# Two transformer blocks on one core: turning order at two norms, turning of memory tokens, pairs in the spatial mixing, and the queue of the modulation loads

## The reference

```python
for layer in range(2):
    mod = silu(c) @ ada_w[layer] + ada_b[layer]           # six rows of 1024
    sh1, sc1, g1, sh2, sc2, g2 = split(mod, 6)
    h = modulate(rmsnorm(x, norm_mix[layer]), sh1, sc1)
    y = retention_mixer(h, ...) if layer == 0 else sgu_mixer(h, ...)
    x = x + g1 * y
    h = modulate(rmsnorm(x, norm_ffn[layer]), sh2, sc2)
    x = x + g2 * peer_ffn(h, ...)
```

## Time and profile before

| | us |
|---|---|
| median of 3 runs | 2386.43 |
| lowest and highest | 2381.01, 2391.15 |
| the profiled execution | 2387.99 |
| its span in the profile | 2386.2 |
| PE busy | 2008.0 (84%) |
| DVE busy | 1578.9 (66%) |
| ACT busy | 1012.5 (42%) |
| POOL busy | 652.3 (27%) |

### The profile page before, as it was taken

How to read it: one execution, slowest core, us unless ns; L and a number is a source line. 1 busy time by engine, 2 the same in 40 slices (tenths; PEclk the granted TensorE clock), 3 DMA queues, 4 the chain that set the end, 5 groups by cost and what they waited for, 6 DMA issues and landing times. The chain is left out here.

```text
span 2386.2 us, 23881 instructions
## 1 busy us (share of the span) xinstructions
PE 2008.0 (84%) x8016; PEld 1248.9 (52%) x8016; DVE 1578.9 (66%) x2973; ACT 1012.5 (42%) x2119; POOL 652.3 (27%) x642
## 2 busy tenths in 40 slices
PE   3998879877877788899877988888878888989998
PEld 2976665322222233379655544434333336868997
DVE  6875766766667676578665766676677655555654
ACT  2342344444444444345333443544454444344543
POOL 0011023443434434110002434443444440400000
PEclk9999999999999999999998999999999999889999
DMA  6785669999999999787455989999999995323553
GB/s 277 285 302 195 218 264 421 421 421 422 421 421 420 422 421 418 295 304 266 148 201 195 421 369 422 411 421 417 421 418 417 421 421 196 124 99 122 184 187 141
DMA packets 112633, 761.92 MB, mean 319 GB/s; under 512 B 12880, under 2 KB 13664, under 8 KB 26368
## 3 DMA queue, kind: packets, MB, share of 16 engines
q0 software_dynamic: 88240, 591.62, 60.8%
q1 hardware_dynamic: 23312, 165.78, 18.8%
q10 hardware_dynamic: 960, 3.01, 0.4%
HBM read 759.32 MB, written 1.05 MB: 319 GB/s over the span
## 5 line engine op out<-in xcount | busy, mean ns | idle before, releaser
L837 PE MATMUL pair<-uv,p_diag 128*128 128x512 f32 x1536 | 755.0, 627 | 188.3 <-ACT p_diag L2005 187.8
L1416 DVE CUSTOM_DVE_ANT_0 uv<-uv,p_h 128x1024 f32<-128x1024 f32 x384 | 470.3, 1225 | 351.2 <-DMA uv<-in_peer_uv,p_idx 350.9
L494 POOL DMA_INDIRECT uv<-in_peer_uv,p_idx x384 | 430.5, 1121 | 721.1 <-PE pair L837 592.2
L837 PEld LDWEIGHTS pair<-uv,p_diag 128*128 128x128 f32 x1536 | 278.1, 195 | 640.1 <-ACT p_diag L2005 377.7
L1084 DVE TENSOR_TENSOR ring_low<-ring,ring_high 128x2048 fp32r<-128x2048 f32 x148 | 336.5, 2288 | 146.5 <-ACT ring_high L1820 144.0
L1820 ACT ACTIVATE ring_high<-ring 128x2048 fp32r<-128x2048 f32 x148 | 278.8, 1908 | 217.0 <-DMA ring<-in_ret_w_in 52.6
L1999 ACT ACTIVATE p_act<-p_dot 128x1 f32<-128x1 f32 x512 | 103.1, 201 | 612.3 <-DVE p_dot L1416 611.0
L642 PE MATMUL pair<-hT_high,ring_high 128*128 128x256 f32 x1056 | 303.9, 288 | 4.7 <-DVE hT_low L1094 3.4
L642 PE MATMUL pair<-hT_low,ring_high 128*128 128x256 f32 x1056 | 298.7, 283 | 0.0
L642 PE MATMUL pair<-hT_high,ring_low 128*128 128x256 f32 x1056 | 298.7, 283 | 0.0
L837 PE MATMUL pair<-uv_high,p_diag 128*128 128x512 f32 x512 | 250.3, 620 | 48.8 <-ACT p_diag L2005 45.0
(11 more groups left out here) (345 smaller groups left out, 2393.1 us busy)
## 6 DMA issues: line engine op xcount, KB each, us to landing
ada<-in_ada_w POOLq DMA_DIRECT2D x50, 512.0 KB, 5.3
ring<-in_ret_w_in SPq DMA_DIRECT2D x24, 1024.0 KB, 6.7
ring<-in_sgu_w_in SPq DMA_DIRECT2D x24, 1024.0 KB, 6.2
ring<-in_peer_w_query SPq DMA_DIRECT2D x16, 1024.0 KB, 4.8
ring<-in_w_up SPq DMA_DIRECT2D x16, 1024.0 KB, 4.9
ring<-in_w_down SPq DMA_DIRECT2D x16, 1024.0 KB, 4.8
mod<-in_ada_w POOLq DMA_DIRECT2D x30, 512.0 KB, 6.4
ring<-in_sgu_w_out SPq DMA_DIRECT2D x12, 1024.0 KB, 4.8
```

What stands on the lines that cost most here:

```text
L494: nc.gpsimd.indirect_dma_start(uv_rows[SLOT[l][s]].rearrange("p a d -> p (a d)"), None, experts, bass.IndirectOffsetOnAxis(ap=p_idx[:, k:k ...
L837: mm = nc.tensor.matmul(acc[:, half, :], p_diag[:, n % DIAGS, :], v[:, half * 512:(half + 1) * 512], start=(k == 0), stop=(k == PICKS - 1))
L1416: V.tensor_tensor_reduce(out=u, in0=u, in1=p_h[:, s // PICKS, :], scale=1.0, scalar=0.0, op0=ALU.mult, op1=ALU.add, accum_out=p_dot[:, n % ...
```

## The change

- In norms 1 and 3 DVE makes the low parts of tile 0 ahead of its wait for tile 1's root (`finish_tile`), and ACT takes tile 0's groups between the roots of tile 0 and tile 1. `FILL` loses its entries for norms 1 and 3. `keep_running` now comes before the first tile of a `turn_rows` call that holds tile 1; this moves the fillers of norm 0 ahead of tile 0.
- The memory tokens are turned at s = 41 (tile 0) and s = 47 (tile 1); ACT takes them at s = 43 and 49, DVE lowers them at s = 44 and 50.
- PE makes a memory block at the ninth step of its unit instead of the first. ACT's high of the later block moves from the start of the unit to k = 10, DVE's low from k = 9 to k = 13.
- In the mixing DVE does the sum and product of b and b + 1, then both low parts, then one ring low. The ring block named at odd b is (b + 1) // 2, at even b it was b // 2 + 1.
- The 80 modulation loads are issued by SP after ring loads that `loaded_after` names: piece j after the ring block two behind the one that goes before the sum of piece j - 3 (j - 2 from piece 48 on). The waits of `load_ada` itself stay.

```diff
+MEM_AT = (41, 47)
-FILL = {0: 3, 1: 3, 2: 4, 3: 3, 5: 6}
+FILL = {0: 3, 2: 4, 5: 6}
...
+        taken_after = []
+        for c in range(12):
+            for n, count in enumerate((0, 0) if c == 0 else (1, 1) if c < 4 else (1, 2) if c < 10 else (2, 2)):
+                taken_after += count * [2 * c + 2 + n]
+        taken_after += 8 * [25] + [26 + n // 2 for n in range(8)]
+        for c in range(12):
+            taken_after += [first_block_of[("sgu_v", 6)] + 2 + 2 * c + n for n in range(2)]
+        taken_after += [first_block_of[("sgu_out", 1)] + 2 + n // 2 for n in range(8)]
+        loaded_after = collections.defaultdict(list)
+        for j in range(len(ADA_AT)):
+            ahead = 3 if j < 6 * KD else 2
+            start = R - 1 if j < 6 * KD else first_block_of[("sgu_v", 6)] + 3
+            loaded_after[max(start, taken_after[j - ahead] + 2 if j >= ahead else 0)].append(j)
...
                 sp.dma_start(ring[:, i % R], blocks[i]).then_inc(w_in[i % R], 16)
+                for j in loaded_after[i]:
+                    if j == 6 * KD:
+                        sp.wait_ge(x_ready, norm_count(2, 1))
+                    load_ada(sp, j)
...
                     load_gain_and_bias(v)
-                    for j in range((v - 2) * KD, (v - 1) * KD):
-                        load_ada(pool, j)
...
+                if TT - 1 in tiles:
+                    keep_running(("hT", n, tiles[0], 0), FILL.get(n, 0))
                 for t in tiles:
-                    if t == TT - 1:
-                        keep_running(("hT", n, t, 0), FILL.get(n, 0))
...
-                        turn_rows(6, m_h)
+                    if l == 1 and s in MEM_AT:
+                        turn_rows(6, m_h, (MEM_AT.index(s),))
...
-                    if l == 1 and s % TOPK == 0 and 0 <= j < 8:
+                    if l == 1 and s % TOPK == TOPK // 2 and 0 <= j < 8:
                         memory_block(j // 2, j % 2)
...
             def finish_tile(n, t, h, shift):
+                if n in (1, 3) and t == 1:
+                    lows_hT(n, ((0, 0), (0, 1)))
...
-                    if b:
-                        us_low(b - 1)
                     dve.wait_ge(small_ready, SMALL[name] + 1)
...
-                    if b >= 2 and b % 2 == 0:
-                        lows(first_block_of[("sgu_out", 0)] + b // 2 + 1)
-                us_low(CU // 2 - 1)
+                    if b % 2:
+                        us_low(b - 1)
+                        us_low(b)
+                        lows(first_block_of[("sgu_out", 0)] + (b + 1) // 2)
...
-                for t in range(TT):
-                    last_half_root(1, t)
+                last_half_root(1, 0)
+                take_hT(1, ((0, 0), (0, 1)))
+                last_half_root(1, 1)
```

More of the change, by code:

```diff
@@ L1420, in peer @@
                 n = 1 + 2 * l
-                lows_hT(n)
+                lows_hT(n, ((1, 0), (1, 1)))
                 first = query_first[l]
@@ L1448, in peer @@
                         if s == 40:
-                            if l == 1:
-                                lows_hT(6)
                             lows(first + 9)
-                        if k == late and l == 1 and KV_UNIT <= i < KV_UNIT + 8:
+                        if l == 1 and s - 3 in MEM_AT:
+                            t = MEM_AT.index(s - 3)
+                            lows_hT(6, ((t, 0), (t, 1)))
+                        if k == 13 and l == 1 and KV_UNIT <= i < KV_UNIT + 8:
                             lows(kv_first + i - KV_UNIT + 2)
@@ L1959, in peer @@
                 n = 1 + 2 * l
-                take_hT(n)
+                take_hT(n, ((1, 0), (1, 1)))
                 def exponentials(i):
@@ L1991, in peer @@
                         did(A.activation(dst, pair[kv_pair][:, :, :], ACT.Copy), kv_taken, c + 1)
-                    if l == 1 and KV_UNIT <= i < KV_UNIT + 8:
-                        highs(kv_first + i - KV_UNIT + 2)
                     for k in range(TOPK):
@@ L2016, in peer @@
                                 take_mod(11)
-                                take_hT(6)
                             highs(first + 9)
+                        if l == 1 and k == 10 and KV_UNIT <= i < KV_UNIT + 8:
+                            highs(kv_first + i - KV_UNIT + 2)
+                        if l == 1 and s - 2 in MEM_AT:
+                            t = MEM_AT.index(s - 2)
+                            take_hT(6, ((t, 0), (t, 1)))
                         if s == EXIT_AT:
@@ L2059, in sgu @@
                     high_of(s_us[0][:, 2 * b:2 * b + 2, :], s_t[:, 4 + 2 * (b % 2):6 + 2 * (b % 2), :])
-                    if b >= 2 and b % 2 == 0:
-                        highs(first_block_of[("sgu_out", 0)] + b // 2 + 1)
+                    if b % 2:
+                        highs(first_block_of[("sgu_out", 0)] + (b + 1) // 2)
                 highs(block_after(("sgu_out",), 0))
@@ L2066, in sgu @@
                 load_keys(1)
-                for t in range(TT):
-                    last_half_root(3, t)
+                last_half_root(3, 0)
+                take_hT(3, ((0, 0), (0, 1)))
+                last_half_root(3, 1)
             def hybrid():
```

## The result

The changed kernel ran at 2359.54 us (median of four, 2355.3 to 2366.3) beside 2385.59 us for the kernel before: ratio 0.9892, 95% interval 0.9860 to 0.9925, so 26 us less. Timed again with the experiments it had 2357.55 us (2355.3 to 2360.6) beside 2387.76, ratio 0.9868 [0.9850, 0.9887], 30 us less. The forecast was 2354.5, in the range 2340 to 2373. The profiled execution took 2357.6 us (span 2355.7).

The account below looks back on a forecast made before the run. Two DMA-bound expert phases with dense stages around them, where PE multiplies or waits for DVE's low parts. 9.9 + 12 + 6 + 1 + 3 = 32 off the profiled 2388, less 1.6 to the median: 2354.5 us, range 2340 to 2373.

Parts of the forecast that it names:

- Part 1: Norms 0, 1 and 3: tile 0's low parts made early, fillers gone; 4.5 plus 2.7 twice, 9.9 us gained.
- PE starts near 47.7 and warm: Norm 0: PE's first product starts near 47.7 instead of 52.67, at full clock; 4.5 us of 5.0 taken.
- Part 2: Mixing in pairs: 8.15 us a pair on DVE instead of 9.87, 7.8 on PE; 12 us gained.
- Part 3: Second expert phase, step 36: memory tokens turned tile by tile remove the 213 GB/s hole; 6 us gained.
- Part 4: Memory blocks at mid-unit: ACT waited 30.4 us for PE's block, DMA lost little; 1 us gained.
- Part 5: 80 modulation loads moved from POOL's to SP's queue: 3 us gained, ends -10 and 6.
- Start of sgu ... Net gain 2: Gating unit's start: the two first modulation rows load with the norm, crowding the bias loads; net 2 us gained.
- step for the last sgu_u chunks: Last sgu_u chunks: ring loads wait 2.3 us later behind rows, absorbed by the ring's lead; 0, ends -1 and 8.
- gain of 2 in sgu_out: Second half of sgu_out: row 76 follows one ring block and lands 2 us earlier, shortening DVE's and PE's waits.
- second rival: Mixing bound by PE's own slots, memory tokens still stall; some 8 to 11 us gained, 2377; chance 0.07.
- rival in which half arrives: PE cold in more first products, mixing ring blocks late, step-36 wait moves to DVE: 13 us gained, 2373; chance 0.13.
- slower rival: SP's ring loads in retention, sgu_u and sgu_out issued late behind row waits: 39 us slower, 2425; chance 0.03.

Follow-up runs that it names:

- the control: The changed kernel once more, unaltered, timed on the same chip in the same rounds as the second group of experiments: 2357.55 us.

## Why the prediction came out right

The forecast of 32 us less stands against 26 and 30 measured. By its steps:

- **Part 1**, 9.9: undoing it costs 7.7 to 9.7. The three starts were right: 47.7 forecast and 47.8 measured; 4.2 earlier forecast behind norms 1 and 3, measured 4.6 (299.42 less 283.9, against 290.00 less 279.1) and 3.9 (1265.52 less 1249.8, against 1238.74 less 1226.9). The 1.5 us for the clock fits norm 1, where 3.3 of the 4.6 reach the gather. In norm 3 only 1.0 of 3.9 does in this profile: 1.5 by the clock and the 1.39 of waiting for the exponentials, which the sum left out and which was 0 to 2.6 us in the profiles of the experiments. One step was wrong: "PE starts near 47.7 and warm". The fillers ran ahead of tile 0, and behind them PE idled 3.56 us between the tiles, where it waits for a slot that DVE's low part frees; the first product then ran at half clock. With fillers in that gap two of three profiles began at full clock and one, with 1.72 us of idling left, at half.
- **Part 2**, 12: 14.7 to 16.7. The mechanism was exact and the size too small. The working gave 14 (62.8 less 48 is in fact 14.8) and I took 2 off, since PE would have little slack. That price for PE was the mis-sized term: PE needs 7.24 us a pair, not 7.8, and the measured cycle of DVE is 7.87 against my 8.15, with the ring's low waiting 1.11 us and no block late. The stage, from the first mixing addition (1137.65) to the result taken (1184.87), is 47.2 us against 62.8: under the 48 to 51 that I named.
- **Part 3**, 6: 5.1 to 7.1, with 6.4 us less from first to last gather (676.7 to 670.3). The price by the rate missing in the window, 7.4, was near.
- **Part 4**, 1: nothing, by one run and its stage. Right in kind: the DMA rate and not ACT's 30.4 us was the thing to read.
- **Part 5**, 3: nothing (-0.8 to 1.2). The step that failed is "Start of sgu ... Net gain 2": the first value row did come 2 us earlier, but PE, which bounds these products, started no earlier and waited as long in sum as before. The step for the last sgu_u chunks, "the ring's lead absorbs that", held on PE up to the mixing in this profile: no wait for a ring low over 0.15 us behind 40 us from the bias issue. What the sum left out is the step behind them, PE's wait for DVE's first addition, 3.0 to 6.3 us where POOL's loads have 1.9. The gain of 2 in sgu_out did not come in the first profile (4.4 us, before 4.3) but came in the control (2.5) and in six others. The landing times are no case against one queue: a modulation row of the `ada` places landed in 5.8 and 5.6 us in the median with SP's loads, in 5.3 and 5.1 with POOL's, but one of the `mod` places in 6.1 and 5.8 against 6.4 and 5.9, and a ring block of the gating unit in 6.9 and 8.3 against 6.2 and 7.1. The Trainium skill (DMA: Bandwidth & Descriptors, Queues, rings and completion order) has each DMA engine take the descriptors of one queue in order, from which I had 2.5 us later per row. Of the two kinds of row one moved that way, by 0.3 to 0.7 us, and the other did not: the size is not borne out.

Low estimate in part 2, high ones in part 5 and for norm 3: the errors were small and of both signs, so the total came nearer than its terms; that much is luck. The second rival ("It doesn't do what it says") has a slip in its own sum, too: parts 1 and 5 make 12.9, not 8 to 11. The rival in which half arrives and the one where the change doesn't do what it says are excluded by the stage times; of the slower rival the mechanism was seen (ring blocks held behind a modulation load, ACT waiting 25.7 us for blocks where it had waited 5.0), in its mildest form: PE had few such waits.

## What to carry to other kernels

Price a stall inside a bandwidth-bound phase by the bytes that its window failed to move (6.7 us here, where the time moved by 5 to 7), never by the wait of an engine: 56 us of waits on ACT were worth nothing. Measure a stage on the engine that bounds it: the first value row, on DVE, came 2 us earlier with each of two edits, and PE started at the same time in both. Where three engines pass one buffer around in a loop, doing two items per turn removes a hand-over for each pair; compare the turn with what the slowest engine needs, and when they agree stop. And when a filler is removed because its place moved, look where the idle gap now lies: the kernel with cheap products put there, in three norms, was 6.5 us faster, though not for a reason that the stages show.

## What was not expected of the hardware

The clock's fall can come after the idle time is over: behind norm 1 with fillers, records went from 0.28 to 0.42 us 0.6 us into dense work, and stayed there for some 3 us. And one program differs from itself by more than the small parts of a sum: retention took 231.3 to 235.7 us in seven profiles of the same code without fillers, the whole changed kernel 2355.3 to 2366.3, and the gating unit 235.8 to 241.9 with the same code in it. A gain of 2 us in such a stage can't be read from a pair of profiles.
